# A two-layer hybrid trunk: chain steps beside the attention units, in four array tiles, and the convolution's part of the output ahead of RWKV's

## The reference

```python
for l in range(2):
    h = rmsnorm(x, norm_w[l]);  proj = h @ w_in[l]          # 1024 -> 4160 columns, four groups of heads
    r, k, v, decay, a = token_shift_mix(proj[RWKV part])    # group 1: RWKV-7 time mixing
    for t in range(512):                                    # per head, a 64 x 64 state
        state = state * w_t - (state @ kk_t) (kk_t * a_t) + v_t k_t
        y_t = state @ r_t
    y_rwkv = head_layernorm(y) * lnx_w + lnx_b + bonus
    y_conv = b_gate * causal_conv3(c_gate * u)              # group 2
    y_moba = blockwise_causal_attention(q, k, v, bias)      # group 3
    y_ret  = rms_per_head(retention(q, k, v))               # group 4
    y = concat(each y * silu(its gate projection));  x = x + y @ w_out[l]
out = rmsnorm(x, final_norm_w)
```

## Time and profile before

| | |
|---|---|
| median of 3 runs | 576.5 us |
| the profiled execution | 576.78 us, span 575.0 us, mean granted TensorE clock 0.997 |
| TensorE busy | 567.4 us, 99% of the span; weight loads 464.0 us |
| VectorE busy | 381.0 us, 66% |
| ScalarE busy | 278.3 us, 48% |
| GpSimd busy | 249.3 us, 43% |
| matmuls of the projections (L772, L774, L775) | 1280, 173.2 + 162.3 + 168.5 us |
| matmuls of the output (L1221 to L1223) | 384, 149.6 us |
| DMA | 64.58 MB, 39.4% of 16 engines' span |

### The profile page before, as it was taken

How to read it: one execution, slowest core, us unless ns; L and a number is a source line. 1 busy time by engine, 2 the same in 40 slices (tenths; PEclk the granted TensorE clock), 3 DMA queues, 4 the chain that set the end, 5 groups by cost and what they waited for, 6 DMA issues and landing times. The chain is left out here.

```text
span 575.0 us, 12739 instructions
## 1 busy us (share of the span) xinstructions
PE 567.4 (99%) x5244; PEld 464.0 (81%) x5244; DVE 381.0 (66%) x644; ACT 278.3 (48%) x555; POOL 249.3 (43%) x197
## 2 busy tenths in 40 slices
PE   9999999999999999999999999999999999999995
PEld 7978888888877777888898788888888777788884
DVE  4999976482488557774543897947537865778163
ACT  5486231343574475534656743324357335735253
POOL 4946552044941323536335455402386313145340
PEclk9999999999999999999999999999999999999998
DMA  9546634056432122353535423332743321224513
GB/s 281 161 130 206 212 97 111 8 130 149 109 79 75 39 75 62 113 171 132 165 117 139 111 77 108 88 70 58 161 127 83 77 73 39 73 75 147 184 40 143
DMA packets 103373, 64.58 MB, mean 112 GB/s; under 512 B 29151, under 2 KB 94227, under 8 KB 103316
## 3 DMA queue, kind: packets, MB, share of 16 engines
q1 hardware_dynamic: 103316, 63.77, 39.4%
HBM read 55.61 MB, written 8.14 MB: 111 GB/s over the span
## 5 line engine op out<-in xcount | busy, mean ns | idle before, releaser
L706 POOL TENSOR_TENSOR w_lo<-w_raw,w_hi 128x512 fp32r<-128x512 f32 x156 | 216.6, 1409 | 283.0 <-ACT w_hi L1295 277.7
L772 PE MATMUL bank<-act_hi,w_hi 128*128 128x512 f32 x432 | 173.2, 401 | 0.0
L775 PE MATMUL bank<-act_lo,w_hi 128*128 128x512 f32 x432 | 168.5, 390 | 0.0
L774 PE MATMUL bank<-act_hi,w_lo 128*128 128x512 f32 x416 | 162.3, 390 | 0.0
L1295 ACT ACTIVATE w_hi<-w_raw 128x512 fp32r<-128x512 f32 x140 | 80.3, 622 | 74.1 <-PE bank L857 28.2
L772 PEld LDWEIGHTS bank<-act_hi,w_hi 128*128 128x128 f32 x432 | 81.1, 188 | 24.7 <-issue 8.2
L775 PEld LDWEIGHTS bank<-act_lo,w_hi 128*128 128x128 f32 x432 | 81.1, 188 | 17.4
L774 PEld LDWEIGHTS bank<-act_hi,w_lo 128*128 128x128 f32 x416 | 78.2, 188 | 14.8
L1221 PE MATMUL bank<-w_hi,act_hi 128*128 128x512 f32 x128 | 50.0, 390 | 0.0
L1223 PE MATMUL bank<-w_hi,act_lo 128*128 128x512 f32 x128 | 49.8, 389 | 0.0
L1222 PE MATMUL bank<-w_lo,act_hi 128*128 128x512 f32 x128 | 49.8, 389 | 0.0
(11 more groups left out here) (217 smaller groups left out, 961.0 us busy)
## 6 DMA issues: line engine op xcount, KB each, us to landing
w_raw<-in_w_in_dram SPq DMA_DIRECT2D x62, 512.0 KB, 4.1
w_raw<-in_w_out_dram SPq DMA_DIRECT2D x16, 512.0 KB, 3.8
pages<-in_x_dram SPq DMA_DIRECT2D x4, 512.0 KB, 6.3
x_or_y<-in_x_dram SPq DMA_DIRECT2D x4, 512.0 KB, 4.2
x_scratch<-x_or_y SPq DMA_DIRECT2D x4, 512.0 KB, 2.9
x_or_y<-x_scratch SPq DMA_DIRECT2D x4, 512.0 KB, 3.7
out_dram<-pages SPq DMA_DIRECT2D x8, 256.0 KB, 2.2
bias_scratch<-pages SPq DMA_DIRECT2D x1, 1280.0 KB, 8.1
```

The costliest lines, as they stand in the source:

```text
L706: ins = pool.tensor_tensor(low, raw, w_hi[:, i % HI, k, 0:n].bitcast(F32), ALU.subtract)
L772: mm(b[:, :], hi, act_hi[:, k, :], start=n == 0, stop=False)
L774: mm(b[:, :], lo, act_hi[:, k, :], start=False, stop=False)
L775: ins = mm(b[:, :], hi, act_lo[:, k, :], start=False, stop=n == KT - 1)
```

## The change

It has five parts.

1. *Chain.* `chain(c)` for c = u + 1 stands in one group with the scores of unit u + 1, that is after the values of unit u - 1, at intervals of two slots (chain 1 with `chunk_h` in `after[12]`). The four matmuls use four array tiles: the second pair of heads writes the other half of the output partitions. They go to two banks, 7 and that one of banks 0 and 1 in which the running projection is not. VectorE takes a whole instruction for the first pair and two of 64 partitions for the second, and the copies of `first_state` and of the chunk decay become three each.
2. *Attention* units from `attend_turn(0)` on stand one slot later. `chunk_q` stands in `after[14]`, `chunk_y1` comes in two steps (one for each pair of heads), in `after[16]` and `after[18]`, and `chunk_y` in `after[24]`.
3. *Layer norm.* `ln_square` moves from slot 21 to 25, `ln_var` from 22 to 26, the four `ln_recip` from 22, 23, 25, 26 to 26, 26, 27, 28, the two `ln_scale` from 26, 27 to 27, 28. `rwkv_finish(0)` moves from slot 28 to behind the first four `split_y`.
4. *Order of the output.* Blocks 2, 3 (convolution) come before blocks 0, 1 (RWKV), in `split_y`, in the last projection, in the rows of `w_out`, and in the rows of x loaded back.
5. *Start.* VectorE waits for nw1 only before the product that reads it; of the idle matmuls, three between nw1 and the transposes go, and three of the four behind them.

```diff
-                    (11, ("chunk_gh",)), (17, ("chunk_y1",)), (21, ("ln_square",)), (22, ("ln_var",))]:
+                    (11, ("chunk_gh",)), (25, ("ln_square",))]:
-    for c in range(1, NCH - 1):
-        if c % 2:
-            mid[12 + c].insert(0, ("chain", c))
-    mid[13].append(("chunk_h",))
...
-            mid[11 + 2 * u].append(("attend_turn", u - 1))
-            after[11 + 2 * u].append(("attend_values", u - 1))
+            mid[12 + 2 * u].append(("attend_turn", u - 1))
+            after[12 + 2 * u].append(("attend_values", u - 1))
...
-        if u in (1, 2, 3):
-            after[11 + 2 * u].append(("chain", 2 * u))
         if u < UNITS:
-            (after[11 + 2 * u] if u else mid[10]).append(("attend_scores", u))
-            (mid[12 + 2 * u] if u else after[11]).append(("attend_norm", u))
-    mid[15][1:1] = [("chunk_q",), ("queries",)]
-    after[19].append(("chunk_y",))
+            after[12 + 2 * u].append(("chain", u + 1))
+            (after[12 + 2 * u] if u else mid[10]).append(("attend_scores", u))
+            (mid[13 + 2 * u] if u else after[11]).append(("attend_norm", u))
+    after[12].append(("chunk_h",))
+    after[14].append(("chunk_q",))
+    mid[15].append(("queries",))
+    after[16].append(("chunk_y1", 0))
+    after[18].append(("chunk_y1", 1))
+    after[24].append(("chunk_y",))
+    after[26].append(("ln_var",))
...
-                    (21, ("conv_taps", 0)), (24, ("conv_taps", 1)), (22, ("ln_recip", 0)), (23, ("ln_recip", 1)), (25, ("ln_recip", 2)), (26, ("ln_recip", 3)),
-                    (26, ("ln_scale", 0)), (27, ("ln_scale", 1)), (28, ("rwkv_finish", 0))]:
+                    (21, ("conv_taps", 0)), (24, ("conv_taps", 1)), (26, ("ln_recip", 0)), (26, ("ln_recip", 1)), (27, ("ln_recip", 2)), (28, ("ln_recip", 3)),
+                    (27, ("ln_scale", 0)), (28, ("ln_scale", 1))]:
...
-    s += [("split_y", k) for k in Y_ORDER[:4]] + [("rwkv_finish", 1), ("split_y", 0), last[-1], ("conv_out", 0), ("split_y", 1), ("conv_out", 1)]
+    s += [("split_y", k) for k in Y_ORDER[:4]] + [("rwkv_finish", 0), last[-1], ("conv_out", 0), ("conv_out", 1), ("split_y", 2), ("split_y", 3), ("rwkv_finish", 1)]
     s += [("split_y", k) for k in Y_ORDER[6:]] + [("out", q) for q in range(5)] + [("out_end",)]
...
-Y_ORDER = [6, 7, 4, 5, 0, 1, 2, 3]
-ROW_ORDER = [3, 2, 0, 1]
+Y_ORDER = [6, 7, 4, 5, 2, 3, 0, 1]
+ROW_ORDER = [3, 2, 1, 0]
...
-            layer.append((f"chain{step[1]}", 7, 1))
+            layer += [(f"chain{step[1]}_0", 7, 1), (f"chain{step[1]}_1", 1 - place_of[projections[-1]], 1)]
...
-            idle(3)
             pe.wait_ge(s("const_a"), 16)
             turn(0, 0)
             turn(1, 0)
-            idle(4)
+            idle(1)
...
-                        pe.wait_ge(*read(f"chain{c - 1}", layer))
-                    b = begin(f"chain{c}", layer)
+                        for p in range(2):
+                            pe.wait_ge(*read(f"chain{c - 1}_{p}", layer))
+                    banks = [begin(f"chain{c}_{p}", layer) for p in range(2)]
                     for p in range(2):
                         for hh in range(2):
-                            r = slice(64 * hh, 64 * hh + 64)
-                            ins = mm(b[r, p * N:(p + 1) * N], GT[r, p, c, :], ST[r, p, c, :], start=True, stop=True)
-                    end(ins, f"chain{c}", layer)
+                            r = head_rows(hh)
+                            ins = mm(banks[p][head_rows(hh ^ p), 0:N], GT[r, p, c, :], ST[r, p, c, :], start=True, stop=True)
+                        end(ins, f"chain{c}_{p}", layer)
...
-            for a in range(2):
-                dve.wait_ge(*full(f"nw{a}", -1))
             for two in (0, 2):
                 for t in (two, two + 1):
                     invert_root(t, 0)
                     for a in range(2):
+                        if t == 0:
+                            dve.wait_ge(*full(f"nw{a}", -1))
...
-                    for p in range(2):
-                        ins = stt(ST[:, p, c + 1, :], b[:, p * N:(p + 1) * N], w_end[:, p, c:c + 1], HP[:, p, c, :], ALU.mult, ALU.add)
-                    ins.then_inc(done(f"chain{c}", layer), 1)
+                    b = [ps(f"chain{c}_{p}", layer) for p in range(2)]
+                    stt(ST[:, 0, c + 1, :], b[0][:, 0:N], w_end[:, 0, c:c + 1], HP[:, 0, c, :], ALU.mult, ALU.add).then_inc(done(f"chain{c}_0", layer), 1)
+                    for hh in range(2):
+                        o = head_rows(1 - hh)
+                        ins = stt(ST[head_rows(hh), 1, c + 1, :], b[1][o, 0:N], w_end[o, 1, c:c + 1], HP[o, 1, c, :], ALU.mult, ALU.add)
+                    ins.then_inc(done(f"chain{c}_1", layer), 1)
```

More of the change, by code:

```diff
@@ L181, in layer_steps @@
         if u > 0:
[L182 to L183 removed]
+            mid[12 + 2 * u].append(("attend_turn", u - 1))
+            after[12 + 2 * u].append(("attend_values", u - 1))
             if u % 3 == 0:
[L185 to L187 removed]
+                after[12 + 2 * u].append(("attend_out", u // 3 - 1))
         if u < UNITS:
[L189 to L195 removed]
+            after[12 + 2 * u].append(("chain", u + 1))
[8 more added lines that the diff above has]
+    after[26].append(("ln_var",))
+    for i, step in [(10, ("ret_recip", 1)), (11, ("ret_recip", 2)), (12, ("ret_recip", 3)), (13, ("ret_finish", 0)), (15, ("ret_finish", 1)),
+                    (21, ("conv_taps", 0)), (24, ("conv_taps", 1)), (26, ("ln_recip", 0)), (26, ("ln_recip", 1)), (27, ("ln_recip", 2)), (28, ("ln_recip", 3)),
+                    (27, ("ln_scale", 0)), (28, ("ln_scale", 1))]:
         after[i].append(step)
@@ L301, in bank_jobs @@
             layer += [("q0", 6, 1), ("q1", 5, 1)]
-        elif kind == "chunk_y1":
+        elif kind == "chunk_y1" and step[1] == 0:
             layer += [("y0", 5, 1), ("y1", 6, 2)]
         elif kind == "chain":
-            layer.append((f"chain{step[1]}", 7, 1))
+            layer += [(f"chain{step[1]}_0", 7, 1), (f"chain{step[1]}_1", 1 - place_of[projections[-1]], 1)]
         elif kind == "retain_scores":
@@ L1080, in chunk_q, with chunk_y1, by_chunk @@
                     by_chunk("q", "q", range(NT))
-                def chunk_y1():
-                    by_chunk("y", "y", range(NT))
-                def by_chunk(what, job, blocks):
+                def chunk_y1(p):
+                    by_chunk("y", "y", range(NT), (p,))
+                def by_chunk(what, job, blocks, pairs=(0, 1)):
                     U, W = UW[:, :, 0, :], UW[:, :, 1, :]
-                    banks = [begin(f"{job}{c}", layer) for c in range(2)]
-                    for p in range(2):
+                    banks = [begin(f"{job}{c}", layer) if 0 in pairs else ps(f"{job}{c}", layer) for c in range(2)]
+                    for p in pairs:
                         for t in blocks:
@@ L1095, in by_chunk @@
                                     r = slice(64 * c, 64 * c + 64)
-                                    o = banks[c][head_rows(hh ^ c if what == "y" else hh), (p * NT + t) * CH:(p * NT + t + 1) * CH]
+                                    o = banks[c][head_rows(hh ^ {"y": c, "h": p}.get(what, 0)), (p * NT + t) * CH:(p * NT + t + 1) * CH]
                                     bet, kap, v = (rows[x][r, t, h * N:(h + 1) * N] for x in ("bet", "kap", "v"))
@@ L1117, in chain @@
                     else:
-                        pe.wait_ge(*read(f"chain{c - 1}", layer))
-                    b = begin(f"chain{c}", layer)
+                        for p in range(2):
+                            pe.wait_ge(*read(f"chain{c - 1}_{p}", layer))
+                    banks = [begin(f"chain{c}_{p}", layer) for p in range(2)]
                     for p in range(2):
                         for hh in range(2):
-                            r = slice(64 * hh, 64 * hh + 64)
-                            ins = mm(b[r, p * N:(p + 1) * N], GT[r, p, c, :], ST[r, p, c, :], start=True, stop=True)
-                    end(ins, f"chain{c}", layer)
+                            r = head_rows(hh)
+                            ins = mm(banks[p][head_rows(hh ^ p), 0:N], GT[r, p, c, :], ST[r, p, c, :], start=True, stop=True)
+                        end(ins, f"chain{c}_{p}", layer)
                 def chunk_y():
-                    pe.wait_ge(*read(f"chain{NCH - 2}", layer))
+                    for p in range(2):
+                        pe.wait_ge(*read(f"chain{NCH - 2}_{p}", layer))
                     for c in range(2):
@@ L1915, in chunk_gh @@
                         dve.wait_ge(*read(f"h{c}", layer))
-                    dve.tensor_copy(ST[:, :, 1, :], HP[:, :, 0, :]).then_inc(s("first_state"), 1)
+                    dve.tensor_copy(ST[:, 0, 1, :], HP[:, 0, 0, :]).then_inc(s("first_state"), 1)
+                    for hh in range(2):
+                        dve.tensor_copy(ST[head_rows(hh), 1, 1, :], HP[head_rows(1 - hh), 1, 0, :]).then_inc(s("first_state"), 1)
                 def chunk_h():
@@ L1931, in chain @@
                 def chain(c):
```

(13 more changed lines are left out.)

10 lines of the change are left out of this document (5 added, 5 removed).

## The result

The changed kernel takes 580.13 us, the median of 4 runs (579.90 to 580.50), beside 576.58 us for 4 runs of the kernel before: 1.0062 of it, with a 95% interval of 1.0045 to 1.0080. Its profiled execution took 579.9 us, span 578.1 us, so 3.1 us more span than before. The forecast was 580.0 us. The sum was right; its parts were not all, and the ledger further down shows which of them cancelled.

The account below looks back on a forecast made before the run. TensorE, busy 567.4 of 575.0 us, was taken as the bound. Stream and start gains of 2.0 us against waits of 2.1 at out(0) and 3.4 at the last weights gave 576.5 + 3.5 = 580.0 us, range 575.2 to 582.0.

Parts of the forecast that it names:

- order and tiles: TensorE's stream: four-tile chain steps gain 1.2 us and fewer changes of tile shape 0.6 us, over both layers.
- waits in the middle: Attention units and chain's second bank: later VectorE work and moved steps cost TensorE nothing, range 0 to 1 us.
- Stall B: Output stage: weights out4 to out7 load 4.35 us later, so TensorE waits at out7; 3.4 us together, bounds 0 and 5.
- start: Kernel start: fewer idle matmuls let transposes come earlier, but GpSimd's chain limits the gain to 0.2 us; upper bound +0.5.
- stall A: At out(0): late layer norm delays conv_g0's tanh and block 6's low part; 1.05 us a layer, 2.1 us for two.
- Tiles: Twelve chain steps on four array tiles: each gains 0.05 to 0.17 us; 1.2 us taken from 0.6 to 2.0.
- rival 3: Chain steps: four tiles give nothing because two row tiles share a bank; 581.2 us, chance 0.07.
- Changes of shape: TensorE's stream: six fewer changes of tile shape over two layers gain 0.6 us, between 0 and 1.0.
- The sign that was named: Slot 10 to the end of slot 26: this stretch was to be shorter by about 1 us in each layer.
- In unit 5 this just holds: Attention unit 5: transposes follow scores by about 5.2 us, norm takes 5.4, second half needed 0.5 later; cost taken as 0.
- rival 1: Output stage: the weights' chain holds, so only the wait at out(0) appears; 576.6 us, chance 0.15.
- Rival 4: Kernel start: TensorE's clock rises later without the idle matmuls, 1.4 to 2.8 us more; some 581.5, chance 0.12 shared with another rival.

Follow-up runs that it names:

- the copy later: Changed kernel with ln_scale(1) in slot 29, conv_taps(0) in slot 23 and ScalarE's scaled copy of conv_h(1) behind unit 5's probability copies: 575.23 us, 0.9979 of the kernel before.
- the tanh first: Changed kernel with only ln_scale(1) moved from slot 28 to 29, behind the first tanh of the convolution's gate: 576.78 us, 1.0003 of the kernel before.
- the rows of x later: Changed kernel with SP's load of the fourth row block of x, and its wait for y_split 8, behind out4 and out5: 577.82 us, 1.0018 of before.
- the start alone: Kernel before with only the start's edit (fewer idle matmuls, later wait for the norm's weights): 575.93 us, 0.9990 of the kernel before.
- both scales later: Changed kernel with both ln_scale in slot 29, conv_taps(0) in slot 23 and the scaled copy of conv_h(1) moved back: 575.47 us, 0.9984 of the kernel before.

## Why the prediction was right, and where by luck

The ledger, profiled execution, both layers, in us. The row "order and tiles" is the lost time of all groups before, 49.01, against 47.30 in the run with the copy later without its `out(0)` (24.01 - 0.34 and 23.96 - 0.33), which has the changed kernel's groups and none of the waits at unit 5. The row of the waits in the middle is the changed kernel's 50.66 without A (0.94 and 0.95), less 47.30. Stall B is 0.74 + 0.86.

| | predicted | measured |
|---|---|---|
| order and tiles in the stream | -1.8 | -1.7 |
| start | -0.2 | 0 in this profile, -0.3 on the mean |
| waits in the middle | 0 (0 to 1) | +1.5 |
| stall A | +2.1 | +1.9 |
| stall B | +3.4 | +1.6 |
| sum | +3.5 | +3.3; span +3.1, medians +3.55 |

*The bound.* Right: busy sums said nothing here, deadlines did. Three engines have a third or more of the time free, and the kernel became slower without any of them becoming the bound.

*Tiles.* Right in size: 0.86 us by two kernels on one chip where 1.2 was taken from 0.6 to 2.0. The passes start (0.34 - 0.22) / 7 = 0.017 us apart, half the distance of two tiles, although the two row tiles of a pair write one bank, in different halves of its partitions. So the full rate that the earlier trace rows showed holds for the chain too, and rival 3, for which the Trainium skill's "TensorEngine Tiling (Array Packing)", Gotcha 1, spoke, fell; the measured distance decides. What was wrong is that this gain reached the end. The third VectorE instruction was booked as free on an engine with a third of its time free.

*Changes of shape.* What the tiles leave of 1.7 us is 0.8, where 0.6 was predicted. No run had the order alone, so this is a remainder, not a measurement, and 0.3 of it is the wait at unit 4's values, 0.17 us in each layer, which the kernel before had and the new order hasn't. The sign that was named, a stretch shorter by about 1 us in each layer, failed: without `out(0)` its groups lose 24.3 us for 24.5, since unit 5 took the gain.

*The failed step: "In unit 5 this just holds".* The sentence counted unit 2's path from scores to norm and took it over. Unit 5 has two things in it that unit 2 hasn't: the taps on VectorE ahead of the scores, and conv_h(1) on ScalarE between norm and copies. A chain step stands ahead of the scores of every unit in the new order; its third instruction shows here, where VectorE is late already. A queue in order must be written out at each place; a like unit elsewhere isn't like where its neighbours differ. The waits came to 1.5 us, outside the 0 to 1 that was given. Its causes are shown by three runs: the taps (0.84 for 1.18 at the turn), the third instruction (0.51 us a layer with two tiles), and ScalarE's copy (2.20 for 2.63).

*Stall A.* Right in mechanism, place and nearly in size: `act_lo[6]` was to start at O - 2.4 + 1.54 + 0.65, some 0.2 us before O; it started at 246.02, 0.08 before 246.10, and `out(0)` lost 0.94 us where 1.05 was said. The 0.35 us that TensorE takes to get going was too long: it went on 0.10 us after the low part here (246.94 to 247.04) and 0.05 us at out7 (277.77 to 277.82). The run with the tanh first took 0.6 of it, and the 0.33 left is, by the trace, the low part's meeting with GpSimd (1.55 us for 0.69). The upper bound had been drawn from such a meeting.

*Stall B: the term that was mis-sized*, 1.6 for 3.4 us. Against the start that `out(0)` could have had, out4's load came 13.70 us later (259.80 - 246.10), before 8.57 (255.44 - 246.87): 5.1 us for the 4.35 that were said, since the last low part was later by so much (2.97 of it is the first low part, 246.02 against 246.10, before 243.82 against 246.87). That should have made B larger. But the rest was shorter than before: from the last low part's start to the end of GpSimd's out7 it took 275.52 - 254.35 = 21.2 us before, and 277.77 - 258.70 = 19.1 us after. Of the 2.1 us, 1.13 are the last four low parts on GpSimd, 5.27 us for 6.40; the rest lies mostly between the load of out4 and its high part, 4.89 us here (264.69 - 259.80) and 5.83 before (261.27 - 255.44); why the load was faster stays open. Here is VectorE in the kernel before, beside the of GpSimd from 269.12 to 275.52:

```profile
269.44 6.64 DVE L2038 TENSOR_TENSOR pages<-x_or_y,pages 128x512 f32<-128x512 f32 x4
```

Four products took 6.64 us there, all beside GpSimd, and 3.15 us in the changed kernel, where they ran mostly while GpSimd stood idle (270.51 to 272.50), and GpSimd's low parts were nearly as fast behind them (5.27) as its four before (5.05). Both engines slow each other down when they meet, and the shift moved them apart. The run with the rows of x later had the meeting back: there four products took 5.79 us and four low parts 6.64. The prediction named this, allowed at most 0.7 us for it and took the middle of 1.65 to 2.35, so 0.35 stands where 2.1 came. The too long 0.35 us of getting going made up another 0.3 us a layer. The Trainium skill, "SBUF — State Buffer", section "SBUF: two separate sides", calls the port pair of VectorE and GpSimd an exclusive lock that a VectorE instruction with two operands from SBUF also needs beside a GpSimd instruction that reads SBUF; the 1.66 us of a product beside GpSimd and 0.79 without agree.

*A and B were not two risks.* The prediction gave rival 1, A without B, a chance of its own. The run with the tanh first removed B with the step that was to mend A, though it took away only 1.8 of the 5.1 us, because B was no deeper than 0.74 and 0.86 us. The hold of A on B was in the text (2.85 of the 4.35 us), so B's chance should have hung on A's size.

*The start.* 0.2 was a little low: 0.5 us by the run alone (0.1 to 1.1 by its interval), where +0.5 was given as the upper bound. The reason for so little was right in part: k0's 13th matmul waited for GpSimd's low part in three of the ten profiles with the edit, until 14.07, 13.82 and 13.79. Rival 4 was real in part too: in the changed kernel's profile the clock rose late and ate the gain (below).

So the total was right by luck in part: the wait that was missed (1.5) and what B was too large by (1.8) cancelled. Had only B been sized right, the same working would have given 578.2 us, and had only unit 5 been seen, 581.5.

## What to carry to other kernels

In queues that run strictly in order, cost a moved step by what it now stands ahead of: here a 0.8 us affine with a table load behind it, one step too early, held the tanh, the splits, SP's wait and four weight tiles, and cost 2.8 us in waits; moving that one entry by one slot brought the time back to that of the kernel before. Look for slack at each place by itself, for an instruction more on an idle engine is free only where nobody waits for that engine. And when two stalls share a cause, give them one chance, and test by removing the cause before mending the stalls.

## What the runs showed of the hardware

*The moment at which TensorE's clock rises differs between executions with the same start.* Timelines of TensorE, the changed kernel and then the run with the tanh first, which has the same instructions up to here. The 256-column matmuls start 0.21 us apart in the first, which is 1.2 GHz, and 0.12 in the second, which is 2.4. In the changed kernel the change came after 13.5 us. The profile's column of the granted clock shows 1.00 in all these stretches, so the distance of the starts has to be read.

```profile
12.29 0.41 PE L817 MATMUL bank<-act_hi,w_lo 128*128 128x256 f32 x1
12.50 0.41 PE L818 MATMUL bank<-act_lo,w_hi 128*128 128x256 f32 x1
```

```profile
12.16 0.28 PE L817 MATMUL bank<-act_hi,w_lo 128*128 128x256 f32 x1
12.29 0.28 PE L818 MATMUL bank<-act_lo,w_hi 128*128 128x256 f32 x1
```

TensorE was busy for 1.36 of the 2 us from 7 to 9 in the one and for 1.32 in the other. The early rise shows 19.85 at the parameters' transposes and the late one 20.35. Of the ten profiles with the start's edit two show the late rise, the changed kernel's and that of the start alone (20.11), and of the three with the idle matmuls none. What decides it stays open, and it isn't all that moves this point: with both scales later the rise was early, k0's 13th matmul waited 0.66 us for GpSimd, and the transposes stood at 20.30.

*A table load is issued ahead of the wait of its activation*: with both affines later it ran at 235.85, and the tanh 2.99 us after it, when its projection was done. So its 1.28 us cost nothing there; in the changed kernel the tanh follows the load at once (242.54 + 1.28, 243.83), and they lie in the path.
